# A state-space branch: own buffers for seven squares, stores asked for sooner, three filling steps fewer before each read-out

## The reference, cut to what matters

```
xn = rmsnorm(x, attn_norm_g)
u_s5 = (xn @ w_in)[..., o3:]                       # 512 channels
y_s5 = s5_mixer(u_s5, ...)                         # scan over time, then gelu
    gl = y @ w_glu;  y = gl[..., :512] * sigmoid(gl[..., 512:])
gate = sigmoid(xn @ w_gate[b])                     # one 1024x1024 product for each branch b
merged += gate * (y_b @ w_branch[b])
```

## Time and profile before

| what | value |
|---|---|
| median of 3 runs (lowest, highest) | 3564.88 us (3564.41, 3566.82) |
| the profiled execution's own time | 3563.29 us |
| its span, first to last instruction | 3561.5 us |
| mean granted TensorE clock in it | 0.983 of full speed |
| busy: PE, DVE, ACT, POOL | 3407.1, 1971.5, 1360.4, 471.8 us |

### The profile page before, as it was taken

How to read it: one execution, slowest core, us unless ns; L and a number is a source line. 1 busy time by engine, 2 the same in 40 slices (tenths; PEclk the granted TensorE clock), 3 DMA queues, 4 the chain that set the end, 5 groups by cost and what they waited for, 6 DMA issues and landing times.

```text
span 3561.5 us, 39577 instructions
## 1 busy us (share of the span) xinstructions
PE 3407.1 (96%) x16116; PEld 2768.4 (78%) x16116; DVE 1971.5 (55%) x2387; ACT 1360.4 (38%) x1899; POOL 471.8 (13%) x332
## 2 busy tenths in 40 slices
PE   8999999999999899999999999999899989999998
PEld 5787888777777578888888877787698768888886
DVE  8454452333554434677773364444676678888335
ACT  3222121433145733433331156343545454444213
POOL 1000000000000000444440010000000035554000
PEclk9999999999999999999999999999999999999999
DMA  3312332111420013233338322120203312324732
GB/s 117 79 36 94 122 136 90 42 48 56 148 78 30 27 49 127 88 113 108 112 132 317 107 77 99 54 101 30 95 1 125 119 71 107 119 107 144 309 103 83
DMA packets 116118, 355.92 MB, mean 100 GB/s; under 512 B 16200, under 2 KB 26184, under 8 KB 115920
## 3 DMA queue, kind: packets, MB, share of 16 engines
q1 hardware_dynamic: 113824, 353.05, 28.2%
q10 hardware_dynamic: 2112, 0.33, 0.1%
HBM read 269.20 MB, written 82.95 MB: 99 GB/s over the span
## 4 chain that ended last, share of the span: by engine, by line
PE 81%; DVE 9%; ACT 7%; issue 1%; DMA 1%; SPq 0%; ACTq 0%; DVEq 0%
PE PS L491 40%; PE PS L2423 21%; PE PS L474 8%; PE PS L3767 1%; PE PS L1906 1%; PE PS L3779 1%; PE PS L2898 1%; ACT whi L431 1%; PE PS L1615 1%; ACT dS L1669 1%; DVE wlo L436 1%; PE PS L991 1%; PE PS L509 1%; PE PS L1928 0%; DVE dO L1733 0%
## 5 line engine op out<-in xcount | busy, mean ns | idle before, releaser
L436 DVE TENSOR_TENSOR wlo<-raw,whi 128x1024 fp32r<-128x1024 f32 (+3 forms) x393 | 497.6, 1267 | 440.7 <-ACT whi L431 437.9
L431 ACT CAST whi<-raw 128x1024 fp32r<-128x1024 f32 (+3 forms) x393 | 372.6, 948 | 758.0 <-PE PS L491 341.5
L491 PE MATMUL PS<-xhi,whi 128*128 128x512 f32 x1872 | 605.7, 405 | 17.5 <-DVE sbVt L2115 6.4
L491 PE MATMUL PS<-xlo,whi 128*128 128x512 f32 x1872 | 583.6, 393 | 0.0
L491 PE MATMUL PS<-xhi,wlo 128*128 128x512 f32 x1872 | 581.6, 392 | 0.0
L491 PEld LDWEIGHTS PS<-xhi,whi 128*128 128x128 f32 x1872 | 348.8, 190 | 104.0 <-issue 15.2
L491 PEld LDWEIGHTS PS<-xlo,whi 128*128 128x128 f32 x1872 | 355.4, 190 | 76.4
L491 PEld LDWEIGHTS PS<-xhi,wlo 128*128 128x128 f32 x1872 | 354.8, 190 | 76.2
L2423 PE MATMUL PS<-tf,whi 128*128 128x512 f32 x936 | 288.2, 389 | 1.7 <-DVE wlo L436 1.7
L2423 PE MATMUL PS<-xhi,whi 128*128 128x512 f32 x624 | 243.9, 391 | 7.2 <-DVE xlo L2408 5.6
L2423 PE MATMUL PS<-xlo,whi 128*128 128x512 f32 x624 | 243.6, 390 | 0.0
(11 more groups left out here) (557 smaller groups left out, 5633.0 us busy)
## 6 DMA issues: line engine op xcount, KB each, us to landing
raw<-in_w_up SPq DMA_DIRECT2D x88, 512.0 KB, 3.3
hid<-hs SPq DMA_DIRECT2D x88, 512.0 KB, 3.6
raw<-in_w_in SPq DMA_DIRECT2D x67, 512.0 KB, 3.3
slot<-hid SPq DMA_DIRECT2D x56, 512.0 KB, 6.8
adr<-in_w_ada SPq DMA_DIRECT2D x48, 512.0 KB, 4.7
raw<-in_w_down SPq DMA_DIRECT2D x48, 512.0 KB, 3.6
raw<-in_w_gate SPq DMA_DIRECT2D x32, 512.0 KB, 3.5
merged<-hid SPq DMA_DIRECT2D x16, 512.0 KB, 12.9
```

The lines of the kernel that those rows point to most:

```text
L431: act.e.copy(whis[i % RING][:, ks, :], raws[i % RING][:, ks, :]).then_inc(*give("w_hi", i))
L436: dve.e.tensor_tensor(wlos[i % RING][:, ks, :], raws[i % RING][:, ks, :], whis[i % RING][:, ks, :].bitcast(F32), ALU.subtract).then_inc(*g ...
L491: ins = pe.e.matmul(ps[:, h * 512:(h + 1) * 512], w[s][:, k, :], x[:, h * 512:(h + 1) * 512], start=(at == 0 and n == 0), stop=(at == kt - ...
```

## The change

Three edits, and a fourth that goes with them:

- The seven squares of half 1 for k = 1 to 7 go into places of their own, the second halves of `xhi` (not yet written then), and the wait for `x_add` is gone.
- SP's store of a gate stands at 8p+7 in place of 8p+11, so ahead of the load at 8p+8; and slot `k` of SP stands ahead of its four `Mk` DMAs in place of behind them.
- Slots: `k` 3 and `ks` 10 (5 and 8), `turn`, `sin`, `rot` 7 each (8 each) in both halves. Slot `glu` is what is left of 104 steps: 12 in place of 6.
- VectorE does the four `gx_lo` (L525) ahead of its part of slot `glu`.

```diff
+        squared = [xrstd[:, half[1]]] + [mem("sqb", base0 + k * TB + TB // 2, [128, 512]) for k in range(1, 8)]
...
                 act.wait_ge(f"away{k}", "x", 1) if hf else act.wait_ge(f"lane{k}", "x")
-                if hf and k >= 4:
-                    act.wait_ge("x_add", k - 3)
-                elif k >= 3 and not hf:
+                if k >= 3 and not hf:
                     act.wait_ge("x_ss", k - 3, 0)
-                into = xtmp[k % 3] if k or not hf else xrstd
-                act.e.activation(into[:, half[hf]], X[:, k, half[hf]], ACT.Square).then_inc(*give("x_sq", k, hf))
+                into = squared[k] if hf else xtmp[k % 3][:, half[0]]
+                act.e.activation(into, X[:, k, half[hf]], ACT.Square).then_inc(*give("x_sq", k, hf))
...
-                pool.e.tensor_tensor(total, total, xtmp[k % 3][:, half[1]], ALU.add).then_inc(*give("x_add", k))
+                pool.e.tensor_tensor(total, total, squared[k], ALU.add).then_inc(*give("x_add", k))
...
-        SLOTS = [("cl", 21), ("k", 5), ("ks", 8)]
+        SLOTS = [("cl", 21), ("k", 3), ("ks", 10)]
...
-            SLOTS += [(f"turn{hf}", 8), (f"sin{hf}", 8), (f"rot{hf}", 8)]
+            SLOTS += [(f"turn{hf}", 7), (f"sin{hf}", 7), (f"rot{hf}", 7)]
...
-            for kind, p in slot_events(slot, 0, 4):
+            for kind, p in slot_events(slot, 0, 0):
...
             beside_sp(sp, "cl")
+            beside_sp(sp, "k")
             sp.wait_ge("s5_ks", 1, 1)
             sp.wait_ge("s5_mzero")
             for q in range(4):
                 s5_rows(sp, q, "s5_mk")
-            beside_sp(sp, "k")
...
-            beside_dve(dve, "glu")
             for f in range(4):
                 dve.wait_ge("gx_hi", f)
                 lo_of(dve, Y[1][:, f, :], U[:, f, :], Y[0][:, f, :], "gx_lo", f)
+            beside_dve(dve, "glu")
```

## The result

The changed kernel takes 3544.72 us (median of 4 runs, 3543.69 to 3546.93) where the kernel before took 3565.85 in the same comparison (4 runs, 3564.41 to 3567.22): ratio 0.9942, interval 0.9924 to 0.9959. The profiled execution took 3544.96 us with a span of 3543.2, against 3563.29 and 3561.5. By these medians the gain is 21.1 us; span against span of the profiled executions it is 18.3 us, where the sum had 16.6.

A forecast was written before the change was run, and what follows sets the result against it. TensorE, busy 3407.1 of 3561.5 us, was taken as the bound, with only idle or low-clock time to win. Terms 6.8 + 7.8 + 2.0 = 16.6 us gave 3544.9 span, 3548.3 us median; range 3543 to 3556.

The forecast's parts named there:

- Squares: Input stage, squares of half 1 without the wait for additions: cost nothing, gain nothing; bounds 1.7 us either way.
- term one: First L509 block of the inputs: earlier by 6.5 us, plus half of 0.8 us slow clock; 6.8 us gained.
- The lower bound's own sum: Earliest `Mk` landing: 104.1 plus 11.6 us (7.9 for 2048 packets, 3.7 for the store ahead), so 115.7.
- rival A: `Mk` DMAs land in time, at 115.7 by rate alone: term one 10.8, time 3544.3 us; chance 0.20.
- term two: Six steps fewer ahead of the read-outs gain 8.21 us, less 0.4 at `w_glu`: 7.8 us.
- Cover of `H`: Time by which `H` is ready before TensorE wants it at the read-outs: 1.5 and 2.7 us.
- term three: First `w_glu` matmuls: no lower clock after 1.2 us of idle, 4.75 - 2.74 = 2.0 us gained.
- B: `Mk` DMAs land late, SP's taking 15.3 us as before: term one 2.5, time 3552.6 us; chance 0.18.
- C: Shorter fill uncovers VectorE, `H` late at read-outs: 3552.3 us, or 3556.5 with all six steps lost; chance 0.09.
- D: Slower: SP's `Mk` DMAs, behind a sigmoid wait, land much later; 3583 us at three times 15.3; chance 0.03.
- E: Change doesn't do what it says: both stalls return in full at the next wait, 3564.9 us; chance 0.03.

The follow-up runs named there:

- the early sigmoid: Changed kernel with ScalarE's sigmoid of gate 2 moved into slot `k`: 3543.36 us; with `w_glu` also starting from PSUM pair 1: 3541.81 us.

## Why the prediction was right, point by point

**The mechanism** was right: two stalls of TensorE behind stores, no other engine's work, and nothing of VectorE uncovered. The old slots of either kind (5.1 and 5.2), the old place of SP's slot `k` (6.1) and, on top of that, the old place of the store (8.9) each cost time when put back. The parts do not add, though. SP's edits alone bring 6.6 us and the slots alone 2.9, together 9.5, where both bring 18: in one kernel the `Mk` DMAs came late, in the other a load stood ahead of the store, and TensorE stood still for that instead.

**Squares: 0.** Right, by their own kernel, and by GpSimd's 11.98 us in one piece.

**Slot `k` and the `Mk` DMAs, term one: 6.8 predicted, 10.0 measured.** This is the term that was mis-sized (its own parts, 6.5 and half of 0.8, add up to 6.9). Its steps up to the issue held (`L938` 0.2 us sooner than I said, SP's four at 105.73 where the middle of my range was 106.3). The landing did not: I took the middle, 119.8, between the pace of one queue and the 15.3 us of the trace before, and it was 117.1. The start accounts for 0.6 us of the 2.7, the time to land for 2.1 (11.4 in place of 13.5). The lower bound's own sum, put on the measured start, gives 105.7 + 11.6 = 117.3. So it came out nearly as rival A had it, but in part by luck, since two misses cancel: the store ahead was in by 108.1, 2.4 us after the first `Mk` DMA was asked, where the sum had 3.7, and the rows took the next 9.1 us, where it had 7.9. The 15.3 us of before was the wrong row to take the middle from: there the rows of both queues ran at once. The packets of two stretches of 8 us show it (queue: packets, MB, share of 16 engines), first of before, then of after; `q10` is ScalarE's queue, `q1` SP's:

```profile
q1 hardware_dynamic: 1370, 0.52, 55.2%
q10 hardware_dynamic: 1251, 0.13, 18.1%
```

```profile
q1 hardware_dynamic: 1471, 0.55, 61.6%
```

Before, ScalarE's queue still had 1251 of its 2112 packets to move while SP's moved 1370; after, ScalarE's rows are done by 108 us. That both were in flight at once is what these rows show. That this made the landing longer is argued and not shown, though the traces order themselves so. ScalarE's four began 0.9 us ahead of SP's in the kernel before and in that with the squares only: 15.3 and 15.7 us from the first of SP's four to the landing of the last. Where they began 3.4 to 4.3 us ahead, it is 13.5 to 13.7 (the changed kernel without SP's edits, that with SP's slot `k` behind the DMAs, and both with the early sigmoid). Where they began 7 to 8 us ahead, it is 11.2 to 12.7. The first two of the middle group have, like the kernel before, one load just ahead of SP's four and no store. In the others a store, or a store and a load, moved as well. By the Trainium skill, page "DMA: Bandwidth & Descriptors", section "Issuing engines are not separate DMA queues", DMAs of several engines run on the same 16 engines and interleave; the trace agrees in that packets of both queues moved in the same 8 us. The section also says that the time to start a DMA is usually small beside the DMA itself. Here it was not small: ScalarE stood still for 4.27 us over four DMAs that took 3.6 to 5.7 us each from issue to landing.

So the stall at that block was 1.01 us where 3.6 was predicted. The clock stayed at its upper level, 1.00, so that the slow stretch of before behind 127.62 was won whole and not by half: block (9.25) and stretch (0.75) make 10.0.

**Steps moved to the end, term two: 7.8 predicted, 7.7 measured.** Cover of `H` 1.5 and 2.7 predicted, 1.7 and 2.9 measured; stall ahead of `w_glu` 1.2 predicted, 1.11 measured. One reason was incomplete: the moved steps need the store's new place. With it alone the stall is 3.90 us (8 steps), with the steps alone 7.11, with both 1.11.

**Clock behind `w_glu`, term three: 2.0 predicted, 1.9 measured.**

**The number.** The three terms measured make 19.6, 3.0 more than the sum. Of this 1.3 did not pass through the later stages, which the prediction had expected to keep the shift whole. The other 1.8 us of the miss of 3.6 come from neither: the prediction put the median 1.59 above the profiled execution, and it lay 0.24 below. That the time fell so close to rival A's is therefore partly luck.

**Rivals.** B was not what happened: it needed 15.3 us to landing. C's mechanism did not occur at 7 or 6 steps, but at 5. There its price of 1.37 us a step was too low, since it had no clock in it: even all twelve steps lost would make 16.4 us, and it was 26. D and E did not occur.

## What to carry to other kernels

When the trace shows a DMA's time from issue to landing, look what else was in flight on the 16 engines before carrying that time over; if the change takes the other traffic away, the time can be shorter (11.4 for 15.3 us here). A store that frees a buffer goes ahead of the load that can wait, and filling work moved into a stall has to be checked for what is queued behind it. When work that covers a wait is shortened, count the cover that is left in us: with 1.7 us left, and even with 0.7 and a wait of 0.37, the cut cost nothing here, and past the cover 8.9 us of waits cost 25, the greater part in TensorE's clock.

## What was unexpected of the hardware

- The four `Mk` DMAs took ScalarE 4.15 us to issue alone, 4.92 and 5.14 beside a load and a store, and 6.88 beside SP's four; SP's took 6.2 to 6.9 alone and 7.8 to 9.1 close upon or beside ScalarE's. From the first issue of SP's to the start of the copy that waits for them it was 11.2 to 12.2 us in the six executions that begin them at about 106 us, after ScalarE's, 12.0 and 12.8 in the two that begin them at 109.8 and 109.2, and 13.5 and 13.7 where they began at 103.4 and 103.3. The 15.3 of the trace before is the last issue and its landing put together, since no copy waited there.
- An idle time of 3.90 us ahead of `w_glu` stood in two kernels, and the clock fell behind it in both, but for unequal times: with SP's edits on the old slots the slow matmuls ended at about 277.5, 3.4 us after the start, with 8 steps at about 272.9, 5.3 us after it.
- Behind idle times of 3.33 and 5.57 us ahead of the read-outs the granted clock stayed at 0.50 for about 17 and 19 us of unbroken work, and rose behind the six products `L491` there. Behind 8.80 us ahead of `w_glu`, the first twelve products took 4.75 us, and the clock was back within them.
